# The second exponential, the angles and the sines of S5 moved behind h

## The reference

```python
cf = silu(c); sh1, sc1, g1, sh2, sc2, g2 = split(cf @ mod_w + mod_b, 6)
h = rmsnorm(x, norm1_g) * (1 + sc1) + sh1
x = x + g1 * mixer(h)              # z = h @ w_in + b_in, then S5, mLSTM, forgetting attention, gates, w_out
h = rmsnorm(x, norm2_g) * (1 + sc2) + sh2
x = x + g2 * (silu(h @ w1) * (h @ w3)) @ w2
```

```python
dt = exp(log_dt)                             # the first exponential
mag = exp(dt * are); ang = dt * aim          # the second exponential, the angles
abar_r, abar_i = mag * cos(ang), mag * sin(ang)
p, q = abar_r - 1, abar_i
coef_r = (p * are + q * aim) / (are**2 + aim**2)
coef_i = (q * are - p * aim) / (are**2 + aim**2)
```

## Time and profile before

| | us |
|---|---|
| median of 3 runs | 882.0 (879.46 to 886.16) |
| profiled execution, its own time | 881.7 |
| its span | 880.0 |
| PE busy | 850.4 (97%) |
| DVE busy | 442.4 (50%) |
| ACT busy | 324.9 (37%) |
| POOL busy | 32.9 (4%) |
| mean granted clock of PE | 0.993 of 2.4 GHz |

### The profile page before, as it was taken

How to read it: one execution, slowest core, us unless ns; L and a number is a source line. 1 busy time by engine, 2 the same in 40 slices (tenths; PEclk the granted TensorE clock), 3 DMA queues, 4 the chain that set the end, 5 groups by cost and what they waited for, 6 DMA issues and landing times.

```text
span 880.0 us, 10526 instructions
## 1 busy us (share of the span) xinstructions
PE 850.4 (97%) x3936; PEld 682.3 (78%) x3936; DVE 442.4 (50%) x719; ACT 324.9 (37%) x477; POOL 32.9 (4%) x46
## 2 busy tenths in 40 slices
PE   3989999999999999999999999999999999999997
PEld 1568888877877777777888878888888888888886
DVE  4789978236779553333883373333333333322222
ACT  4454445442232443433333563333333332222221
POOL 1010000000000000000001110000000000000110
PEclk9899999999999999999999999999999999999999
DMA  8923322347884211215323323333333333333322
GB/s 302 292 68 89 89 75 74 92 153 233 283 282 150 67 53 48 67 30 167 89 80 120 95 64 99 99 97 95 95 95 95 95 95 90 90 107 90 96 77 96
DMA packets 149372, 100.67 MB, mean 114 GB/s; under 512 B 11072, under 2 KB 142552, under 8 KB 148312
## 3 DMA queue, kind: packets, MB, share of 16 engines
q1 hardware_dynamic: 146080, 100.10, 37.3%
q10 hardware_dynamic: 3256, 0.10, 0.2%
HBM read 97.03 MB, written 2.10 MB: 113 GB/s over the span
## 4 chain that ended last, share of the span: by engine, by line
PE 90%; DVE 4%; ACT 2%; issue 1%; DMA 1%; SPq 1%; POOL 0%; DVEq 0%; ACTq 0%
PE bank L1608 25%; PE bank L1610 25%; PE bank L1609 25%; PE bank L1625 2%; PE bank L1819 2%; PE bank L1749 1%; PE bank L1841 1%; PE bank L1769 1%; PE bank L1780 1%; DMA modA<-in_mod_w 1%; PE bank L1866 1%; PE bank L1832 1%; PE bank L1817 1%; DVE wlo L1115 1%; ACT whi L631 1%
## 5 line engine op out<-in xcount | busy, mean ns | idle before, releaser
L1608 PE MATMUL bank<-h_lo,whi 128*128 128x512 f32 x712 | 285.6, 401 | 4.8 <-DVE wlo L1115 2.6
L1610 PE MATMUL bank<-h_hi,wlo 128*128 128x512 f32 x712 | 278.2, 391 | 0.0
L1609 PE MATMUL bank<-h_hi,whi 128*128 128x512 f32 x712 | 277.9, 390 | 0.0
L1608 PEld LDWEIGHTS bank<-h_lo,whi 128*128 128x128 f32 x712 | 134.1, 188 | 34.7 <-issue 4.4
L1609 PEld LDWEIGHTS bank<-h_hi,whi 128*128 128x128 f32 x712 | 134.2, 189 | 28.8 <-issue 1.7
L1610 PEld LDWEIGHTS bank<-h_hi,wlo 128*128 128x128 f32 x712 | 134.1, 188 | 28.8
L1115 DVE TENSOR_TENSOR wlo<-raw,whi 128x1024 fp32r<-128x1024 f32 x61 | 74.5, 1223 | 103.3 <-ACT whi L631 103.3
L631 ACT ACTIVATE whi<-raw 128x1024 fp32r<-128x1024 f32 x61 | 64.3, 1055 | 156.4 <-PE bank L1610 115.8
L1610 PE MATMUL bank<-a_hi,wlo 128*128 128x512 f32 x176 | 68.5, 389 | 0.0
L1608 PE MATMUL bank<-a_lo,whi 128*128 128x512 f32 x176 | 68.5, 389 | 0.0
L1609 PE MATMUL bank<-a_hi,whi 128*128 128x512 f32 x176 | 68.5, 389 | 0.0
(11 more groups left out here) (326 smaller groups left out, 996.6 us busy)
## 6 DMA issues: line engine op xcount, KB each, us to landing
raw<-in_ffn_w SPq DMA_DIRECT2D x60, 512.0 KB, 3.8
raw<-in_w_in SPq DMA_DIRECT2D x44, 512.0 KB, 4.0
slab<-in_mod_w SPq DMA_DIRECT2D x32, 512.0 KB, 5.7
modA<-in_mod_w SPq DMA_DIRECT2D x4, 1024.0 KB, 11.0
modB<-in_mod_w SPq DMA_DIRECT2D x4, 1024.0 KB, 19.7
raw<-in_w_out SPq DMA_DIRECT2D x8, 512.0 KB, 3.7
raw<-in_ffn_w SPq DMA_DIRECT2D x8, 384.0 KB, 3.2
xtok<-in_x SPq DMA_DIRECT2D x4, 512.0 KB, 5.0
```

Of the source, the lines that this page charges most:

```text
L1608: mm(dst, w_h, m_l, start=first, stop=False)
L1609: mm(dst, w_h, m_h, start=False, stop=False)
L1610: return mm(dst, w_l, m_h, start=False, stop=last)
```

## The change

36 DVE operations on 128 x 8 numbers leave the head: `DT*are`, the whole second `exact_exp` (MAG, EM1), the angle and its reduction (ANG, TH), THP, TLO and the fourth power M4. They become a function `transition()`, called in step 1 right in front of `coefficients()`. The two sines on ACT (SN, SH) with their wait for `s_scal` go from in front of the copies of the transposed x to step 1, behind `hi(2)` and in front of `hi(3)`. Four small scalings of biases (`bq8`, `ngh`, `hb`) stay in the head. The number of instructions on DVE is the same.

```diff
@@ ACT
-            act.wait_ge(s_scal, 1)
-            A(sp[:, SN], sp[:, TH], ACT.Sin).then_inc(s_trig, 1)
-            A(sp[:, SH], sp[:, TH], ACT.Sin, scale=0.5).then_inc(s_trig, 1)
...
             for t in range(1, S_F1):
                 if t >= 3:
                     hi(t)
+                if t == 1:
+                    act.wait_ge(s_scal, 1)
+                    A(sp[:, SN], sp[:, TH], ACT.Sin).then_inc(s_trig, 1)
+                    A(sp[:, SH], sp[:, TH], ACT.Sin, scale=0.5).then_inc(s_trig, 1)
@@ DVE
-            tt(c_(T3), c_(DT), are, ALU.mult)
-            exact_exp(c_(MAG), c_(EM1), c_(T3))
...
-            tt(c_(M4), c_(MAG), c_(MAG), ALU.mult)
-            tt(c_(M4), c_(M4), c_(M4), ALU.mult)
...
+            def transition():
+
+                tt(c_(T3), c_(DT), are, ALU.mult)
+                exact_exp(c_(MAG), c_(EM1), c_(T3))
+
+                tt(c_(ANG), c_(DT), aim, ALU.mult)
+                ts(c_(KQ), c_(ANG), 1.0 / TWO_PI, MAGIC, ALU.mult, ALU.add)
+                ts(c_(KQ), c_(KQ), MAGIC, None, ALU.subtract)
+                for part in (C1, C2, C3):
+                    stt(c_(ANG), c_(KQ), -part, c_(ANG), ALU.mult, ALU.add)
+                V.tensor_scalar(c_(TH), c_(ANG), -3.1415925, 3.1415925, ALU.max, ALU.min).then_inc(s_scal, 1)
+                dve.wait_ge(s_scal, 1)
+
+                ts(c_(THP), c_(TH), 1.0 / TWO_PI, None, ALU.mult)
+                link(V.tensor_copy(th_hi_r[:], c_(THP)))
+                ts(c_(TLO), f_hi, -C1, None, ALU.mult)
+                tt(c_(TLO), c_(TLO), c_(TH), ALU.add)
+                for part in (C2, C3):
+                    stt(c_(TLO), f_hi, -part, c_(TLO), ALU.mult, ALU.add)
+                V.tensor_scalar(c_(TLO), c_(TLO), 1.0 / TWO_PI, None, ALU.mult).then_inc(s_scal, 1)
+                dve.wait_ge(s_scal, 2)
+
+                tt(c_(M4), c_(MAG), c_(MAG), ALU.mult)
+                tt(c_(M4), c_(M4), c_(M4), ALU.mult)
@@ DVE, the steps
                 if t == 1:
+                    transition()
                     coefficients()
```

More of the change, by code:

```diff
@@ L999, in _ @@
                 V.tensor_scalar(xtok[:, t], xtok[:, t], rstd[:, t:t + 1], None, ALU.mult).then_inc(s_xn, 1)
-            tt(c_(T3), c_(DT), are, ALU.mult)
-            exact_exp(c_(MAG), c_(EM1), c_(T3))
[L1004 to L1013, removed]
-            f_hi = th_hi_r[:].bitcast(F32)
[L1015 to L1020, removed]
+            f_hi = th_hi_r[:].bitcast(F32)
             def angles(i):
```

## The result

| | before | changed |
|---|---|---|
| median, us | 882.1 (879.46 to 886.16, 4 runs) | 895.7 (892.43 to 896.62, 4 runs) |
| ratio | | 1.0122, 95% interval 1.0089 to 1.0155 |
| profiled execution, its own time | 881.7 | 895.6 |
| its span | 880.0 | 893.7 |
| mean granted clock | 0.993 | 0.979 |

The changed kernel is slower, by 1.2% as the ratio has it. The ratio times 882.1 is 892.9, inside the stated range by 0.1 us; the median itself, 895.7, lies above its end of 893. The two medians of this table stand at 1.0154 to each other, more than the ratio's interval reaches: 895.7 / 1.0122 is 884.9, close to the 884.1 that the kernel before had over 71 runs in the experiments, while the four runs of this table lie 2 us lower. Run again later, the changed kernel gave a ratio of 1.0096 (1.0059 to 1.0134). So it is clearly slower, and whether by over 1% stays open.

What follows compares the result with a forecast made beforehand. PE, busy for 97% of the span, was taken as the bound. Head 0, DVE 7.28, sines 0 and clock 0 on 881.7 gave 889.0, or 889.3 on the median; range 886 to 893 us.

Steps and rivals of the forecast that it cites:

- The head gives nothing: Head: removing the 36 operations gains 0 us, since DVE's work there stands beside PE's chain; `modc` starts at 41.75 as before.
- 7.28 us on DVE: In front of `coefficients()`: the 36 serial operations take 7.28 us as in the head, so chunk 3 starts at 73.34.
- The stall behind POOL's clearing: Second DVE operation at the new place: the existing stall of 1.17 us stays and is paid once.
- The sines hidden: ACT in step 1: sines done at 60.50, before DVE's 62.03; `hi(3)` and chunk 0's evacuation queue covered; cost 0, at most 0.3 us.
- Nothing later takes the delay back: From chunk 3 on: PE and DVE both stay 7.28 us later, and nothing recovers it.
- The clock: PE's waits before chunks 2 and 3: restart at half clock costs 0 to 2.6 us; taken as 0 for chunk 3.
- Rival 1: Chunk 3 starts at half clock after its wait: 1.6 to 2.6 us on top, 890.6 to 891.6; chance 0.30.
- the upper bound of 2.6 us: Most that a restart at half clock behind PE's wait was said to cost (1.76 + 0.88).
- The wait for `fz`: PE ahead of chunk 2: grows from 1.2 to 5.7 us, with the added 4.5 us inside the 7.28.

Runs made afterwards that it cites:

- the filled kernel: Changed kernel plus 12 spare PE products, results unread, ahead of chunk 2 and 12 ahead of chunk 3, in PE's two waits: ratio 1.0053, median 889.0 us.
- kernels with both waits filled: Spare PE products ahead of chunks 2 and 3, in the changed kernel (ratio 1.0053, median 889.0) and in the kernel before (ratio 0.9969, median 881.0).
- before, again: The kernel before, unchanged, run once more for a second trace of its clock: one run of 885.3 us.

## Why the prediction was right, and where not

**The head gives nothing: shown.** `modc` started at 41.90 against 41.75 (the chain of the earlier trace rows ends at 41.73), and with the operations left out altogether the ratio is 0.9996.

**7.28 us on DVE: shown.** The 36 operations and the stall took from 53.72 to 62.18, 8.46 us, where 7.28 + 1.17 = 8.45 had been worked out. The stall behind POOL's clearing was paid once. Chunk 3 started 7.45 us later, 0.15 of it from the head.

**The sines hidden: shown, with its condition.** TH started at 60.14 (60.00 forecast), the second sine ended at 60.65, the coefficients began at 62.18 without a wait. Chunk 2 started at 62.32 (62.2 forecast). That its cover is `lo(3)` was shown by taking the cover away: the wait for `fz` then cost PE 5.2 us, and putting the sines and tables elsewhere brought the ratio from 1.0074 to 1.0033.

**Nothing later takes the delay back: shown.** PE's later waits are those of before one by one (1.4, 1.3, 0.7, 0.7 and 0.4 us), and chunk 8 of the filled kernel is 7.3 us late like its chunk 3.

**The clock: the step that failed.** It was worked out that a fall in the first wait would lengthen chunk 2 and shorten the second wait to 2.8 to 3.8 us, and that a wait so short would keep the clock. The first half came about as written (2.9 us). The second did not: in both traces of the changed kernel the clock fell about 1 us behind the start of chunk 3. So the term that was put at 0 measured 1.6 us. The reason given was the earlier trace rows, where a wait of 2.6 us had kept the clock. But this wait came behind 5.7 us of dense work at full clock, and the 2.9 us came behind a chunk that ran mostly at half clock, so they weren't alike. The kernel with the operations left out bears on this: its wait of 2.8 us, nearly the same length, came behind a chunk at full clock and was followed by no fall. That the slow chunk is the reason is argued from these traces; no run varied it alone. Rival 1, with a chance of 0.30, was the better description of the cost: its price was 1.6 to 2.6 us. By the Trainium skill, "TensorE: Matmul & The Clock Gate", Part 1 (The HAM clock gate), half rate is the default of an idle array, and the prediction had worked out from it that chunk 3 would start cold. The traces agree behind the waits of 9.2, 9.4 and 4.8 us (0.80, 0.79 and 0.80 us for the first product); behind the 2.9 us chunk 3 started warm (0.50) and the clock fell a microsecond later.

Two readings behind this step were loose. The window from 60 to 66 us lies in front of the end of the 2.6 us wait; the one behind it, 66 to 70, reads 1.00 as well, so nothing hangs on it. And the upper bound of 2.6 us came from products at 15 us that took twice as long as their like later. The profile's clock column reads 1.00 there, so no run shows that this was the clock; the restarts that the column does show, in front of chunk 3 and chunk 4, cost 1.5 to 1.8 us up to chunk 7 or 8.

**The wait for `fz`: 4.6 instead of 5.7 us.** The forecast took the end of chunk 1 as in the trace of before. The half clock of the head lasted 3 us longer in this trace, chunk 1 ended 1.2 us later, and the wait shrank by this. Both lengths of this stretch occur in traces of the kernel before, so it isn't a product of the change.

**The term that was missing.** The forecast took the clock of the rest of the program as given. The single trace of before, at 0.993, is one of the luckier executions: the 71 runs of that kernel in the experiments have clocks from 0.983 to 0.995 and a median of 884.1 us, and 7 of them reach 0.993. The falls behind 230 us come and go from trace to trace, also of one kernel; the first trace of the changed kernel lost about 4.6 us by those at 317 and 385, and that of before had neither. Most of the gap between 889.3 and 895.7 is this: 1.6 us at chunk 3 and some 5 us of later falls, in runs whose clock (0.979 in the trace, 0.980 on average) was below what the same kernel showed later (0.983, median 892.6). The forecast gave 0.33 to "over 1%" and 0.65 to "within 1%". The ratio says 1.2%, its interval reaches down to 0.9%, and the second set gave 1.0%, so the runs don't decide this.

**What was luck.** The delay of 7.28 us was right to 0.1 us and for the reason given. That the result fell inside the range was not earned by the sum: the ratio on the base of 882.1 ends 0.1 us under the upper bound of 893, which had been drawn for rival 1 and scatter, and the forecast had no term for the later falls.

What stays open is why kernels with both waits filled also show fewer falls much later. All three of their traces are without one at 370 to 390 us, and nine of the eleven other traces have one there. Among these nine is the kernel with `lo(3)` early and only the wait of 1.2 us filled. The falls near 263 us in the kernel before and near 385 in the changed one follow groups of products of one column (L1866 and L1872, 12 and 16 of them), but the filled kernels have the same groups and no fall at 385. The runs don't tell what connects a place at 60 us with one at 380.

## What to carry to other kernels

Serial small operations cost their full row on the path of whoever waits behind them: here 36 of them at 0.2 us each were free beside PE's chain in the head and cost 7.3 us in front of one subtraction that PE needed. Before such work is moved, look at what stands behind it on its engine, and move the urgent instruction ahead of it: that alone gave 2.8 us. Where an engine's wait grows, put a price on its clock in this wait and in the next dense piece, and compare kernels over many runs, or by the starts of stages behind a common mark, rather than by the time of one trace.

## What the runs showed of the hardware

Executions of one kernel differ by up to 9.6 us (879.14 to 888.75 over 71 runs of the kernel before), mostly along with the granted clock: at 0.983 they took 888.6 us on average, at 0.989 883.8, at 0.993 880.9. A wait of 9.2 us left chunk 3 at half clock for 3.7 us of work. Waits of 2.9 and 3.1 us behind a slow chunk were followed by a fall a microsecond into dense work, in the two traces of the changed kernel. Waits of 2.6 us (before), 1.4 (before, again) and 2.8 (operations left out), each behind a chunk at full clock, were followed by none. One DVE operation on 128x8 numbers took 1.34 us instead of 0.17 while POOL's clearing of `qpad` ran, in the kernel before; in the changed one the pair of operations at this place took 1.55 us, where the same pair in the head had taken 0.38.
